# Weighted sum of expert rows moved to TensorE, bias and variance scaling moved from GpSimd to VectorE

## Chip, cores, metric

One core of one Trainium2 chip. The metric is the device time of one launch in microseconds; lower is better.

## The reference, cut to what matters

One layer of a streaming encoder for 1024 prompt frames and 64 sample frames (1088 rows of 1024 numbers, fp32). A mixer of retention and attention, then a hierarchical mixture of 16 experts in which every row goes to two experts, then a last layer norm:

```
combine[row, e] = weight of expert e for this row      # two of the 16 are not zero
ffn[row]  = sum over e of combine[row, e] * (silu(h @ w_gate[e]) * (h @ w_up[e])) @ w_down[e]
x[row]    = layer_norm(alpha * x1[row] + gate * ffn[row], ln_ffn_g, ln_ffn_b)
```

Here alpha is 2 ** 0.25, gate is a vector of 1024 (one for the prompt, one for the sample), and the layer norm subtracts the row's mean, multiplies by (variance + 1e-5) ** -0.5, then applies gain and bias.

## The kernel before

The program is written engine by engine, with explicit semaphores; each engine runs its own instructions in order. Earlier stages: modulation, projections, retention, attention, out projection, router. Then the experts work on blocks of 128 rows sorted by expert. ScalarE stores each block of expert results to DRAM (expert_rows, 512 KB a block, L1332).

The final stage is the one that is changed. It goes over nine tiles t of rows: eight of 128 and the last of 64. For tile t:

- GpSimd gathers, by two indirect DMAs (`gather`, L1854), the rows of the first and of the second chosen expert into ya[t] and yc[t]. Their landing counts on semaphore s_y0[t % 4].
- ScalarE multiplies ya[t] by the first weight w0 (L1345), and counts s_crs.
- VectorE adds w1 times yc[t] (L1758), multiplies by the gate row (L1759), adds alpha times x1 while it accumulates the row sum (L1760), and makes the negated mean (L1761), which counts s_cve.
- ScalarE squares the centred rows into yc and accumulates (L1350), s_csq.
- GpSimd scales that sum to variance plus epsilon (L1872), raises it to -0.5 (L1873), multiplies by the negated mean (L1874), s_cnm.
- ScalarE applies scale and shift (L1356), s_cxh; VectorE multiplies by the gain (L1766), s_cg; GpSimd adds the bias (L1879), s_cy; SyncE stores the tile (L749).

The order is fixed by three software pipelines, each a loop over t. VectorE, iteration t: the first part of tile t, then the gain of tile t-3. ScalarE: scaling of t, squares of t-1, application of t-3. GpSimd: gathers of tiles 0, 1, 2 ahead of the loop; in iteration t the gather of t+3 (from t = 1 on after the squares of t-1), the scalars of t-1, the bias of t-3.

TensorE has no work in this stage; its last instruction is L1113. `mm` (L762) is its matrix product helper, so products of all stages have the line L762. The wrapper `step` makes an engine wait for its own instruction; `done` does the same on a named semaphore.

Of the kernel before, what the change touches and what calls it, by code (L numbers as in the profile page):

```python
# [107 lines left out]
def rows_of(t):  # L108
    return P if t < LAST else DEC
# [18 lines left out]
def stream_step(nc, a):  # L128
# [5 lines left out]
    with ExitStack() as ctx:  # L134
# [75 lines left out]
        def tiny(*dims, dt=F32):  # L210
# [74 lines left out]
        gate_lin = view(r_tmp + 1024, 2, 512)  # L285


        s_rot, s_const, s_rows, s_router = sem("rotations_in"), sem("const_in"), sem("rows_in"), sem("router_in")
        s_xb = [sem(f"x_in{i}") for i in range(3)]
        s_adaB = [sem(f"ada_first_in{i}") for i in range(4)]  # L290
        s_adaM = [sem(f"ada_later_in{i}") for i in range(2)]
        s_win = [sem(f"win_in{i}") for i in range(2)]
        s_wout, s_state = sem("wout_in"), sem("state_in")
        s_dv, s_po = sem("dve_steps"), sem("pool_steps")
        s_pH, s_pL = sem("operand_high"), sem("operand_low")
        s_rowT, s_colv, s_csig, s_silu = [sem(n) for n in
# [39 lines left out]
        s_gu, s_sg, s_g1, s_a, s_at, s_aH, s_aL, s_yp, s_ye, s_ys = [sem(n) for n in  # L336
            ("gate_up_ready", "gate_sig", "gate_silu", "act_ready", "act_turned", "act_high", "act_low",
             "down_ready", "y_copied", "y_stored")]
        s_frow = sem("final_rows_in")
        s_y0 = [sem(f"y_gathered{i}") for i in range(4)]  # L340
        s_x1i = sem("x1_in")
        s_cve, s_crs, s_cnm, s_cxh, s_cg, s_cy = [sem(n) for n in
            ("fin_variance", "fin_first", "fin_shift", "fin_applied", "fin_gained", "fin_ready")]
        s_csq = sem("fin_squares")
        s_cacc, s_yo = sem("fin_sum"), sem("y_out")
        s_go = sem("queue_order")
        s_fill = sem("unused_rows_cleared")
# [156 lines left out]
        ya = [view(r_b + D * t, D) for t in range(TILES)]  # L504
        yc = [view(r_a + D * t, D) for t in range(TILES)]
        x1c = [view(r_m + D * t, D) for t in range(TILES)]


        rt = [r_tmp]
# [74 lines left out]
        def _(sp):  # L584
# [78 lines left out]
                                 ).then_inc(s_kc[1], 16)  # L663

            load_cache(0)
            sp.dma_start(wout, w_out[0].rearrange("(k p) n -> p k n", p=P)).then_inc(s_wout, 16)
            for pair in range(1, PAIRS):
                load_cache(pair)

# [51 lines left out]
            for slot, src in enumerate((mod_row(1, 0, 2), mod_row(1, 1, 2),  # L721
                                        ln_ffn_g[0].unsqueeze(0).to_broadcast([P, D]),
                                        ln_ffn_b[0].unsqueeze(0).to_broadcast([P, D]))):
                sp.dma_start(rows8[:, slot, :], src).then_inc(s_frow, 16)

            sp.wait_ge(s_route, 1)
            total = sp.value_load(table[0:1, 16:17], min_val=1, max_val=MAX_BLOCKS - 1)
# [30 lines left out]
        def _(pe):  # L758
# [245 lines left out]
            pe.wait_ge(s_ov, N_OUT + PAIRS)  # L1004
            pe.wait_ge(s_meA, 12)
            pe.wait_ge(s_meD, 12)
            pe.wait_ge(s_wout, 16)

            def h2_turned(t):
                r = rows_of(t)  # L1010
# [64 lines left out]
            with pe.Fori(0, EXPERTS // 2) as ee:  # L1075
                for k in range(2):
                    first = pe.value_load(table[0:1, bass.ds(2 * ee + k, 1)], min_val=0, max_val=MAX_BLOCKS - 1)
                    end = pe.value_load(table[0:1, bass.ds(2 * ee + k + 1, 1)], min_val=1, max_val=MAX_BLOCKS - 1)
                    with pe.Fori(first, end) as b:
                        pe.wait_ge(s_hL, b + 1)  # L1080
                        for half in range(2):
                            pe.wait_ge(s_wL, 12 * ee + 6 * k + 2 * half + 2)
                            for w in range(2):
                                cols = slice(half * 256, half * 256 + 256)
                                for c in range(KC):
                                    last = split_products(bank(half)[:, w * 256:w * 256 + 256], h_high[:, c, :],
                                                          h_low[:, c, :], high_w[w][:, c, cols], low_w[k][w][:, c, cols],
                                                          c == 0, c == KC - 1)
                            last.then_inc(s_gu, 1)
                        for half in range(2):  # L1090
                            pe.wait_ge(s_a, 2 * b + half + 1)
                            for f in range(2):
                                last = nc.tensor.transpose(bank(6 + half)[:, f * P:(f + 1) * P],  # L1093
                                                           an[:, half, f * P:(f + 1) * P], ident)
                            last.then_inc(s_at, 1)
                            if half == 0:
                                pe.wait_ge(s_hg, 16 * b + 32)
                                for c in range(KC):
                                    last = nc.tensor.transpose(psum[1][:, c // 4, (c % 4) * P:(c % 4 + 1) * P],
                                                               hg[:, c * P:(c + 1) * P], ident)  # L1100
                                last.then_inc(s_htr, 1)
                        pe.wait_ge(s_ye, b + 1)
                        pe.wait_ge(s_wL, 12 * ee + 6 * k + 6)
                        for f in range(FC):
                            if f % 2 == 0:
                                pe.wait_ge(s_aL, 2 * b + f // 2 + 1)
                            for hh in range(2):
                                cols = slice(hh * 512, hh * 512 + 512)
                                last = split_products(psum[2][:, hh, :], a_high[:, f, :], a_low[:, f, :],
                                                      high_w[2][:, f, cols], low_w[k][2][:, f, cols], f == 0, f == FC - 1)  # L1110
                        last.then_inc(s_yp, 1)

                    nc.tensor.transpose(bank(7)[0:64, 0:64], ident[0:64, 0:64], ident[0:64, 0:64]).then_inc(s_edone, 1)  # L1113


        @block.scalar
        def _(act):
# [222 lines left out]

            for t in range(TILES + 3):
                if t < TILES:
                    r = rows_of(t)
                    act.wait_ge(s_y0[t % 4], 32 * (t // 4 + 1))
                    A(ya[t][0:r], ya[t][0:r], ACT.Copy, scale=w0[0:r, t:t + 1]).then_inc(s_crs, 1)  # L1345
                v = t - 1
                if 0 <= v < TILES:
                    r = rows_of(v)
                    act.wait_ge(s_cve, v + 1)
                    A(yc[v][0:r], ya[v][0:r], ACT.Square, bias=fin_nm[0:r, v:v + 1],  # L1350
                      accum_out=fin_sq[0:r, v:v + 1]).then_inc(s_csq, 1)
                v = t - 3
                if v >= 0:
                    r = rows_of(v)
                    act.wait_ge(s_cnm, v + 1)
                    A(ya[v][0:r], ya[v][0:r], ACT.Identity, bias=ln_nmr[0:r, v:v + 1],  # L1356
                      scale=ln_rstd[0:r, v:v + 1]).then_inc(s_cxh, 1)
# [3 lines left out]
        def _(dve):  # L1361
# [386 lines left out]
            dve_pair(EXPERTS // 2 - 1, True)  # L1748


            dve.wait_ge(s_frow, 64)
            dve.wait_ge(s_x1i, 16 * TILES)
            for t in range(TILES + 3):
                if t < TILES:
                    r = rows_of(t)
                    x = ya[t][0:r]
                    dve.wait_ge(s_crs, t + 1)
                    step(STT(x, yc[t][0:r], w1[0:r, t:t + 1], x, ALU.mult, ALU.add))  # L1758
                    step(TT(x, x, rows8[0:r, int(t == LAST)], ALU.mult))  # L1759
                    done(STT(x, x1c[t][0:r], ALPHA, x, ALU.mult, ALU.add, accum_out=fin_nm[0:r, t:t + 1]), s_cacc, t + 1)  # L1760
                    done(TS(fin_nm[0:r, t:t + 1], fin_nm[0:r, t:t + 1], -1.0 / D, None, ALU.mult), s_cve, t + 1)  # L1761
                v = t - 3
                if v >= 0:
                    r = rows_of(v)
                    dve.wait_ge(s_cxh, v + 1)
                    TT(ya[v][0:r], ya[v][0:r], rows8[0:r, 2], ALU.mult).then_inc(s_cg, 1)  # L1766


        @block.gpsimd
        def _(pool):  # L1770
# [86 lines left out]
                    pool.indirect_dma_start(dst[0:r], None, y_dram,  # L1857
                                            bass.IndirectOffsetOnAxis(ap=slot_i[0:r, kk, t:t + 1], axis=0)).then_inc(s_y0[t % 4], 16)

            for t in range(3):  # L1860
                gather(t)
            pool.wait_ge(s_frow, 64)
            for t in range(TILES + 3):
                if t + 3 < TILES:
                    if t:
                        pool.wait_ge(s_csq, t)
                    gather(t + 3)
                v = t - 1
                if 0 <= v < TILES:
                    r, c = rows_of(v), slice(v, v + 1)  # L1870
                    pool.wait_ge(s_csq, v + 1)
                    step(G.tensor_scalar(fin_sq[0:r, c], fin_sq[0:r, c], 1.0 / D, EPS, ALU.mult, ALU.add))  # L1872
                    step(G.tensor_tensor(ln_rstd[0:r, c], fin_sq[0:r, c], mhalf[0:r, 0:1], ALU.pow))  # L1873
                    G.tensor_tensor(ln_nmr[0:r, c], fin_nm[0:r, c], ln_rstd[0:r, c], ALU.mult).then_inc(s_cnm, 1)  # L1874
                v = t - 3
                if v >= 0:
                    r = rows_of(v)
                    pool.wait_ge(s_cg, v + 1)
                    G.tensor_tensor(ya[v][0:r], ya[v][0:r], rows8[0:r, 3], ALU.add).then_inc(s_cy, 1)  # L1879


def launch_shapes():
# [31 lines left out]
```

## Time and profile before

| what | value |
|---|---|
| median of 3 runs | 1600.95 us (1599.82 to 1601.17) |
| profiled execution, span | 1600.7 us (its time as a whole isn't shown apart from the span) |
| TensorE busy | 1418.3 us, 89% |
| VectorE busy | 933.1 us, 58% |
| ScalarE busy | 612.9 us, 38% |
| GpSimd busy | 245.9 us, 15% |
| first gather of the final stage starts | 1520.66 us |

The engines are called PE (TensorE), PEld (its weight loads), DVE (VectorE), ACT (ScalarE), POOL (GpSimd) and SP (SyncE) in the rows. Busy shares are means over the whole span. The granted clock is the share of 2.4 GHz that TensorE was given; 0.50 is 1.2 GHz. A time in a row counts from the span's start unless it says otherwise.

### The profile page before, as it was taken

The page shows a single profiled execution, that of the slowest core. Times are in us where ns is not written, and L with a number is a line of the kernel's source. Part 1 is how long each engine was busy: PE and PEld are TensorE (multiplying, and loading weights), DVE is VectorE, ACT ScalarE, POOL GpSimd, SP SyncE. Part 2 cuts the span into 40 slices and gives each one's busy share as a digit, 9 for nine tenths or more (in the row PEclk, how much of TensorE's full clock was granted, in tenths as well). Part 3 has the DMA queues.
Part 4 walks back from the last instruction along what each step waited for, and adds up shares of the span by engine and source line. Part 5 has one row for each costly group of instructions (what it writes and reads, how often), then busy time and mean ns, then how long its engine had stood idle before and what let it go on. Part 6 is the DMA issues. An engine that isn't in the chain of part 4 may idle for free.

```text
span 1600.7 us, 20719 instructions
## 1 busy us (share of the span) xinstructions
PE 1418.3 (89%) x7419; PEld 1004.3 (63%) x7420; DVE 933.1 (58%) x1308; ACT 612.9 (38%) x1054; POOL 245.9 (15%) x239
## 2 busy tenths in 40 slices
PE   5989899998999999999999973799999999999800
PEld 1433333566777666666645543699888889998700
DVE  5486873134611288888745555455888451538676
ACT  0200000124222277777602223145777442437543
POOL 0123210001300000002014430100000000000078
PEclk9999999999999999999999995799999999999955
DMA  9614140101021441211263214555899551539663
GB/s 344 221 53 158 54 164 1 53 1 67 0 86 43 83 138 28 54 27 27 90 226 119 88 64 169 197 210 210 333 381 383 214 211 64 210 116 371 254 220 114
DMA packets 137844, 233.89 MB, mean 146 GB/s; under 512 B 56536, under 2 KB 58144, under 8 KB 137784
## 3 DMA queue, kind: packets, MB, share of 16 engines
q1 hardware_dynamic: 127656, 196.39, 35.2%
q0 software_dynamic: 6352, 23.07, 4.2%
q10 hardware_dynamic: 3776, 13.67, 2.1%
q8 instruction: 34, 0.56, 0.1%
q14 instruction: 26, 0.21, 0.0%
HBM read 197.42 MB, written 35.68 MB: 146 GB/s over the span
## 4 chain that ended last, share of the span: by engine, by line
PE 77%; DVE 12%; POOL 4%; DMA 2%; ACT 1%; issue 1%; SPq 1%; POOLq 0%; DVEq 0%; ACTq 0%
PE psum L762 72%; DVE arena L1512 4%; PE psum L949 3%; POOL arena L1879 1%; DMA arena<-in_w_ada_mix 1%; POOL arena L1857 1%; PE psum L1093 1%; DVE arena L1728 1%; DVE arena L1730 1%; ACT arena L1318 1%; POOL smalls L1873 1%; DVE arena L1513 1%; DVE smalls L1469 1%; DVE arena L1510 1%; PE psum L795 0%
## 5 line engine op out<-in xcount | busy, mean ns | idle before, releaser
L762 PE MATMUL psum<-arena 128*128 128x64 f32 (+10 forms) x1468 | 352.0, 386 | 10.4 <-DVE arena L1699 9.0
L762 PEld LDWEIGHTS psum<-arena 128*128 128x128 f32 (+3 forms) x1468 | 203.2, 189 | 98.5 <-issue 80.1
L762 PE MATMUL psum<-high,h_high 128*128 128x256 f32 x832 | 238.3, 286 | 2.5 <-DVE h_low L1715 2.5
L762 PE MATMUL psum<-high,h_low 128*128 128x256 f32 x832 | 236.6, 284 | 0.0
L762 PE MATMUL psum<-win,hT 128*128 128x512 f32 (+1 forms) x432 | 193.0, 601 | 0.5 <-ACT hT L1131 0.5
L762 PEld LDWEIGHTS psum<-high,h_high 128*128 128x128 f32 x832 | 160.8, 193 | 4.3 <-issue 2.9
L762 PEld LDWEIGHTS psum<-high,h_low 128*128 128x128 f32 x832 | 160.8, 193 | 0.0
L762 PEld LDWEIGHTS psum<-win,hT 128*128 128x128 f32 (+1 forms) x432 | 78.2, 185 | 110.8 <-issue 106.6
L1553 DVE TENSOR_TENSOR_SCAN arena<-arena 128x512 f32<-128x512 f32 (+4 forms) x116 | 115.3, 994 | 26.8 <-ACT arena L1241 24.9
L762 PE MATMUL psum<-low_even,h_high 128*128 128x256 f32 x416 | 118.9, 286 | 0.0
L762 PE MATMUL psum<-low_odd,h_high 128*128 128x256 f32 x416 | 117.7, 283 | 0.0
L1710 DVE TENSOR_TENSOR low_odd<-raw_odd,high 128x2048 fp32r<-128x2048 f32 x48 | 107.9, 2288 | 11.4 <-ACT high L1291 11.3
L1710 DVE TENSOR_TENSOR low_even<-raw_even,high 128x2048 fp32r<-128x2048 f32 x48 | 107.7, 2287 | 10.2 <-ACT high L1291 10.2
L1728 DVE TENSOR_TENSOR arena<-arena,psum 128x256 f32<-128x256 f32 x52 | 21.8, 419 | 145.7 <-ACT arena L1313 95.8
L762 PE MATMUL psum<-win_high,x_high 128*128 128x512 f32 (+1 forms) x216 | 86.8, 402 | 10.0 <-DVE win_low L1492 6.2
L1291 ACT ACTIVATE high<-raw_odd 128x2048 fp32r<-128x2048 f32 x48 | 89.2, 1911 | 6.1 <-ACT arena L1330 6.1
L1291 ACT ACTIVATE high<-raw_even 128x2048 fp32r<-128x2048 f32 x48 | 88.9, 1909 | 5.3 <-ACT arena L1330 5.3
L1512 DVE SCALAR_TENSOR_TENSOR arena<-arena,smalls 128x512 f32<-128x512 f32 x96 | 86.3, 899 | 3.4
L762 PE MATMUL psum<-win_low,x_high 128*128 128x512 f32 (+1 forms) x216 | 85.6, 396 | 0.0
L762 PE MATMUL psum<-win_high,x_low 128*128 128x512 f32 (+1 forms) x216 | 85.5, 396 | 0.0
L762 PE MATMUL psum<-high,a_high 128*128 128x512 f32 x208 | 83.2, 400 | 0.0
L762 PE MATMUL psum<-arena,smalls 128*2 128x512 f32 (+3 forms) x168 | 61.0, 474 | 25.0 <-DMA arena<-in_w_ada_mix 12.5
(227 smaller groups left out, 2301.2 us busy)
## 6 DMA issues: line engine op xcount, KB each, us to landing
raw_even<-in_w_e_gate SPq DMA_DIRECT2D x8, 2048.0 KB, 10.4
raw_even<-in_w_e_up SPq DMA_DIRECT2D x8, 2048.0 KB, 16.9
raw_even<-in_w_e_down SPq DMA_DIRECT2D x8, 2048.0 KB, 15.5
raw_odd<-in_w_e_gate SPq DMA_DIRECT2D x8, 2048.0 KB, 10.2
raw_odd<-in_w_e_up SPq DMA_DIRECT2D x8, 2048.0 KB, 16.3
raw_odd<-in_w_e_down SPq DMA_DIRECT2D x8, 2048.0 KB, 14.7
win<-in_w_in SPq DMA_DIRECT2D x7, 2048.0 KB, 9.2
expert_rows<-arena ACTq DMA_DIRECT2D x26, 512.0 KB, 6.7
```

The costliest lines, as they stand in the source:

```text
L762: pe_last[0] = nc.tensor.matmul(*x, **y)
L949: last = nc.tensor.transpose(bank(3 + u % 2)[0:r, j * P:(j + 1) * P], wgt[:, u % 3, j * P:j * P + r], ident)
L1093: last = nc.tensor.transpose(bank(6 + half)[:, f * P:(f + 1) * P], an[:, half, f * P:(f + 1) * P], ident)
L1291: A(chunk(high_w, c), chunk(raw_w[k], c), ACT.Copy).then_inc(s_wH, 1)
L1318: A(sg[:, 1], bank(1)[:, 0:256], ACT.Sigmoid).then_inc(s_sg, 1)
L1469: TT(rope_a[0:r].rearrange("p h (a d) -> p h a d", a=2), b4, cos, ALU.mult).then_inc(s_ra, 1)
L1510: step(TS(o, w[:, 0], silu_c[:, 0, st:st + 1], None, ALU.mult))
L1512: step(STT(o, w[:, k], silu_c[:, k, st:st + 1], o, ALU.mult, ALU.add))
L1513: done(STT(o, w[:, KC - 1], silu_c[:, KC - 1, st:st + 1], o, ALU.mult, ALU.add), s_acc, i + 1)
L1553: done(V.tensor_tensor_scan(pbr, om[:, u % 3, w - 1::-1], om[:, u % 3, w - 1::-1], init, ALU.mult, ALU.min), s_scan, u + 1)
L1710: TT(chunk(low_w[k], c), chunk(raw_w[k], c), chunk(high_w, c).bitcast(F32), ALU.subtract).then_inc(s_wL, 1)
L1728: TT(an[:, half], sg[:, half], bank(half)[:, 0:256], ALU.mult).then_inc(s_g1, 1)
```

## The change

TensorE makes the weighted sum: for each tile ScalarE writes two 128x128 matrices that hold w0 and w1 of the tile on their diagonal (the identity times a column), and TensorE multiplies them with the gathered rows, in fp32, into one of three PSUM buffers (psum 0, 2, 3, in turn). VectorE reads the sum from PSUM in its gate product. The variance scaling and the bias addition go from GpSimd to VectorE. The GpSimd loop is rewritten: gather t in iteration t, then the scalars of tile t-2. Two semaphores are merged with others: the final rows count on the router's, the output weights on the state's.

The core of the diff:

```
 TensorE, new, behind the experts:
+            for t in range(TILES):
+                r = rows_of(t)
+                pe.wait_ge(s_dg, 2 * t + 2)
+                pe.wait_ge(s_y0[t % 4], 32 * (t // 4 + 1))
+                if t >= 3:
+                    pe.wait_ge(s_cg, t - 2)
+                for hh in range(2):
+                    for kk, y in enumerate((ya[t], yc[t])):
+                        last = mm(fin_psum[t % 3][0:r, hh, :], row_weight[t % 2][0:r, kk, 0:r], y[0:r, hh * 512:hh * 512 + 512],
+                                  start=(kk == 0), stop=(kk == 1))
+                last.then_inc(s_crs, 1)
 ScalarE:
-                    act.wait_ge(s_y0[t % 4], 32 * (t // 4 + 1))
-                    A(ya[t][0:r], ya[t][0:r], ACT.Copy, scale=w0[0:r, t:t + 1]).then_inc(s_crs, 1)
+                    if t >= 2:
+                        act.wait_ge(s_crs, t - 1)
+                    for kk, w in enumerate((w0, w1)):
+                        A(row_weight[t % 2][:, kk], ident, ACT.Copy, scale=w[:, t:t + 1]).then_inc(s_dg, 1)
 VectorE:
                     dve.wait_ge(s_crs, t + 1)
-                    step(STT(x, yc[t][0:r], w1[0:r, t:t + 1], x, ALU.mult, ALU.add))
-                    step(TT(x, x, rows8[0:r, int(t == LAST)], ALU.mult))
+                    done(TT(x, fin_psum[t % 3][0:r].rearrange("p a b -> p (a b)"), rows8[0:r, int(t == LAST)], ALU.mult),
+                         s_cg, t + 1)
                     done(STT(x, x1c[t][0:r], ALPHA, x, ALU.mult, ALU.add, accum_out=fin_nm[0:r, t:t + 1]), s_cacc, t + 1)
                     done(TS(fin_nm[0:r, t:t + 1], fin_nm[0:r, t:t + 1], -1.0 / D, None, ALU.mult), s_cve, t + 1)
+                v = t - 1
+                if 0 <= v < TILES:
+                    r, c = rows_of(v), slice(v, v + 1)
+                    dve.wait_ge(s_csq, v + 1)
+                    TS(fin_sq[0:r, c], fin_sq[0:r, c], 1.0 / D, EPS, ALU.mult, ALU.add).then_inc(s_cvar, 1)
                 v = t - 3
                 if v >= 0:
                     dve.wait_ge(s_cxh, v + 1)
-                    TT(ya[v][0:r], ya[v][0:r], rows8[0:r, 2], ALU.mult).then_inc(s_cg, 1)
+                    step(TT(ya[v][0:r], ya[v][0:r], rows8[0:r, 2], ALU.mult))
+                    TT(ya[v][0:r], ya[v][0:r], rows8[0:r, 3], ALU.add).then_inc(s_cy, 1)
 GpSimd:
-            for t in range(3):
-                gather(t)
-            pool.wait_ge(s_frow, 64)
-            for t in range(TILES + 3):
-                if t + 3 < TILES:
-                    if t:
-                        pool.wait_ge(s_csq, t)
-                    gather(t + 3)
-                v = t - 1
-                if 0 <= v < TILES:
+            for t in range(TILES + 2):
+                if t < TILES:
+                    if t >= 4:
+                        pool.wait_ge(s_crs, t - 3)
+                    gather(t)
+                v = t - 2
+                if v >= 0:
                     r, c = rows_of(v), slice(v, v + 1)
-                    pool.wait_ge(s_csq, v + 1)
-                    step(G.tensor_scalar(fin_sq[0:r, c], fin_sq[0:r, c], 1.0 / D, EPS, ALU.mult, ALU.add))
+                    pool.wait_ge(s_cvar, v + 1)
                     step(G.tensor_tensor(ln_rstd[0:r, c], fin_sq[0:r, c], mhalf[0:r, 0:1], ALU.pow))
                     G.tensor_tensor(ln_nmr[0:r, c], fin_nm[0:r, c], ln_rstd[0:r, c], ALU.mult).then_inc(s_cnm, 1)
-                v = t - 3
-                if v >= 0:
-                    r = rows_of(v)
-                    pool.wait_ge(s_cg, v + 1)
-                    G.tensor_tensor(ya[v][0:r], ya[v][0:r], rows8[0:r, 3], ALU.add).then_inc(s_cy, 1)
```

## Rows read from the trace of the kernel before

**Rows 1.** Head of the page: span, then busy us by engine.

```profile
span 1600.7 us, 20719 instructions
PE 1418.3 (89%) x7419; PEld 1004.3 (63%) x7420; DVE 933.1 (58%) x1308; ACT 612.9 (38%) x1054; POOL 245.9 (15%) x239
```

**Rows 2.** Chain of waits, 1480 to 1601: start us, us, what.

```profile
1520.66 0.94 POOL arena L1857
...
1521.90 5.30 DMA arena<-expert_rows,smalls
...
1594.39 2.29 POOLq L134
```

**Rows 3.** Busy time by stretch: PE, PEld, DVE, ACT, POOL, clock, DMA share, GB/s.

```profile
1540.00:1550.00 10.00, 0.00 (x0) 0.00 (x0) 9.65 (x15) 7.17 (x9) 8.68 (x10) 0.50 0.46 138
```

**Rows 4.** Groups, shapes apart, 1516 to 1601: busy us, mean ns, idle before.

```profile
L1857 POOL DMA_INDIRECT arena<-expert_rows,smalls x18 | 21.0, 1168 | 36.2 <-DMA expert_rows<-arena 28.5 <-issue 4.2 <-ACT arena L1350 3.6
L1879 POOL TENSOR_TENSOR arena<-arena 128x1024 f32<-128x1024 f32 x8 | 20.7, 2596 | 0.0
```

**Rows 5.** Timeline, 1515 to 1601: start us, us, engine, line, operation.

```profile
1529.83 1.23 DVE L1759 TENSOR_TENSOR arena<-arena 128x1024 f32<-128x1024 f32 x1
...
1532.36 0.15 DVE L1761 TENSOR_SCALAR smalls<-smalls 128x1 f32<-128x1 f32 x1
...
1539.64 0.79 POOL L1874 TENSOR_TENSOR smalls<-smalls 128x1 f32<-128x1 f32 x1
...
1541.95 0.94 POOL L1857 DMA_INDIRECT arena<-expert_rows,smalls  x1 [0.30 <-issue]
...
1543.34 1.57 POOL L1873 TENSOR_TENSOR smalls<-smalls 128x1 f32<-128x1 f32 x1
...
1546.01 1.24 ACT L1356 ACTIVATE arena<-arena,smalls 128x1024 f32<-128x1024 f32 x1
...
1546.13 1.90 POOL L1857 DMA_INDIRECT arena<-expert_rows,smalls  x1 [0.16 <-ACT arena L1350]
...
1549.77 0.57 POOL L1873 TENSOR_TENSOR smalls<-smalls 128x1 f32<-128x1 f32 x1
...
1575.27 3.41 DVE L1760 SCALAR_TENSOR_TENSOR arena<-arena 64x1024 f32<-64x1024 f32 x1
...
1584.32 0.19 POOL L1874 TENSOR_TENSOR smalls<-smalls 128x1 f32<-128x1 f32 x1
...
1588.78 7.91 POOL L1879 TENSOR_TENSOR arena<-arena 128x1024 f32<-128x1024 f32 x3
```

**Rows 6.** Line 1857, the two gathers issued at 1546.13 and 1548.34.

```profile
DMA to landing us min/median/max: 5.2/5.3/5.4
```

**Rows 7.** Timeline of weight loads in the out projection, 806 to 811.

```profile
809.47 0.33 PEld L762 LDWEIGHTS psum<-arena 128*128 128x128 f32 x1 [0.52 <-issue]
810.32 0.19 PEld L762 LDWEIGHTS psum<-arena 128*128 128x128 f32 x1 [0.51 <-issue]
810.75 0.19 PEld L762 LDWEIGHTS psum<-arena 128*128 128x128 f32 x1 [0.24 <-issue]
```

**Rows 8.** Busy time by short stretch; the third number from the end is the clock.

```profile
386.00:387.00 1.00, 0.78 (x2) 0.72 (x3) 1.00 (x3) 1.00 (x3) 0.00 (x0) 0.50 1.05 387
...
390.00:391.00 1.00, 1.00 (x4) 0.80 (x4) 1.00 (x2) 0.00 (x0) 0.00 (x0) 0.77 0.45 172
...
1012.00:1014.00 2.00, 1.49 (x7) 1.50 (x8) 2.00 (x2) 1.27 (x1) 0.29 (x1) 0.50 1.06 238
...
1018.00:1019.00 1.00, 1.00 (x8) 1.00 (x8) 0.97 (x1) 0.00 (x0) 0.00 (x0) 0.74 1.04 418
...
1520.00:1521.00 1.00, 0.00 (x0) 0.00 (x0) 0.00 (x0) 0.00 (x0) 0.34 (x1) 0.64 0.00 0
```

**Rows 9.** Line 1739 (ns min/median/max), and a group of ScalarE (us, ns).

```profile
L1739 DVE TENSOR_TENSOR h_low<-psum,h_high x26: 1224/1225/1227, 1030.1 to 1511.4; 128x1024 fp32r<-128x1024 f32 x26
...
L1212 ACT ACTIVATE arena<-psum 128x128 f32<-128x128 f32 x32 | 8.9, 277 | 4.9 <-PE psum L762 4.9
```

More of the change, by code:

```diff
@@ L285, in stream_step @@
         gate_lin = view(r_tmp + 1024, 2, 512)
-        s_rot, s_const, s_rows, s_router = sem("rotations_in"), sem("const_in"), sem("rows_in"), sem("router_in")
+        s_rot, s_const, s_rows, s_router = sem("rotations_in"), sem("const_in"), sem("rows_in"), sem("router_then_final_rows_in")
         s_xb = [sem(f"x_in{i}") for i in range(3)]
@@ L292, in stream_step @@
         s_win = [sem(f"win_in{i}") for i in range(2)]
-        s_wout, s_state = sem("wout_in"), sem("state_in")
+        s_state = sem("state_then_wout_in")
         s_dv, s_po = sem("dve_steps"), sem("pool_steps")
@@ L338, in stream_step @@
              "down_ready", "y_copied", "y_stored")]
-        s_frow = sem("final_rows_in")
         s_y0 = [sem(f"y_gathered{i}") for i in range(4)]
@@ L344, in stream_step @@
         s_csq = sem("fin_squares")
+        s_cvar, s_dg = sem("fin_variance_scaled"), sem("row_weights_ready")
         s_cacc, s_yo = sem("fin_sum"), sem("y_out")
@@ L506, in stream_step @@
         x1c = [view(r_m + D * t, D) for t in range(TILES)]
+        fin_psum = [psum[0], psum[2], psum[3]]
+        row_weight = [view(r_b + D * TILES + 256 * i, 2, P) for i in range(2)]
         rt = [r_tmp]
@@ L665, in _ @@
             load_cache(0)
-            sp.dma_start(wout, w_out[0].rearrange("(k p) n -> p k n", p=P)).then_inc(s_wout, 16)
+            sp.dma_start(wout, w_out[0].rearrange("(k p) n -> p k n", p=P)).then_inc(s_state, 16)
             for pair in range(1, PAIRS):
@@ L723, in _ @@
                                         ln_ffn_b[0].unsqueeze(0).to_broadcast([P, D]))):
-                sp.dma_start(rows8[:, slot, :], src).then_inc(s_frow, 16)
+                sp.dma_start(rows8[:, slot, :], src).then_inc(s_router, 16)
             sp.wait_ge(s_route, 1)
@@ L1006, in _ @@
             pe.wait_ge(s_meD, 12)
-            pe.wait_ge(s_wout, 16)
+            pe.wait_ge(s_state, 32)
             def h2_turned(t):
@@ L1342, in _ @@
                 if t < TILES:
-                    r = rows_of(t)
-                    act.wait_ge(s_y0[t % 4], 32 * (t // 4 + 1))
-                    A(ya[t][0:r], ya[t][0:r], ACT.Copy, scale=w0[0:r, t:t + 1]).then_inc(s_crs, 1)
+                    if t >= 2:
+                        act.wait_ge(s_crs, t - 1)
+                    for kk, w in enumerate((w0, w1)):
+                        A(row_weight[t % 2][:, kk], ident, ACT.Copy, scale=w[:, t:t + 1]).then_inc(s_dg, 1)
                 v = t - 1
@@ L1748, in _ @@
             dve_pair(EXPERTS // 2 - 1, True)
-            dve.wait_ge(s_frow, 64)
+            dve.wait_ge(s_router, 128)
             dve.wait_ge(s_x1i, 16 * TILES)
```

## The prediction, made before the changed kernel was run

> **What bounds the kernel now.** Read the head of the page first [rows 1]: TensorE is busy 89% of the span, GpSimd 15%. That average says nothing of the stage that is changed, because TensorE has finished when it begins. So read next the chain of waits from 1517 us to the end [rows 2]: after the gather of tile 0 (landing at 1527.2) it goes from one GpSimd line to the next, the last one a closing wait at 1594.39. The stage is 80.0 us long, from the first gather's start at 1520.66 to 1600.7. The stretch 1540 to 1550 [rows 3] shows VectorE 9.65 and GpSimd 8.68 of 10 us busy, ScalarE 7.17, TensorE nothing and a granted clock of 0.50. The groups of the stage [rows 4] say what fills GpSimd: 18 gathers (21.0 us) and the bias additions of L1879 (20.7 us in 8, the ninth 2.3). The timeline [rows 5] shows VectorE and GpSimd holding each other up: the 128x1 power L1873 takes 1.57 us beside VectorE work and 0.57 alone, a gather 1.90 or 0.94. So the stage is bound by GpSimd, with VectorE close behind.
>
> **Outside the stage** only semaphores are shared differently (output weights with the state, final rows with the router). Each old wait keeps its position and its transfer, so I take 0. The later count cannot be passed early, since its transfers are issued behind the earlier ones; cover would be missing only if they landed out of order.
>
> **Costs inside the stage, by engine.**
> GpSimd loses 9 bias additions (2.3 to 3.4 us each) and 9 one-column scalings. Per tile it keeps two gathers and two one-column operations: 0.57+0.07+0.19 = 0.85 us with VectorE idle, 1.57+0.07+0.79 = 2.4 us beside it [rows 5].
> VectorE loses the weighted sum L1758 and gets the bias addition (1.23 as L1759) and the scaling (0.15 as L1761). Its gate product now reads PSUM; the nearest row, 128x1024 from PSUM, has 1.225 us [rows 9]. Up to the negated mean an iteration takes 1.25+1.25+0.2 = 2.7 us (1529.83 to 1532.52); with the variance scaling 2.9; gain and bias of the tile three back 2.5. That is 5.4 us per tile.
> ScalarE's 1.15 us scaling becomes two of 128x128. The nearest row, 128x128 from PSUM without a scale column, has 0.277 us [rows 9]; bounds are that and 1.15, the operation replaced; I take 0.3. They are written an iteration ahead, during the gather's flight; uncovered, 0.3 to 2.3 us a tile.
> TensorE gets, per tile, four products 128x128 by 128x512 in fp32. The weight loads of the out projection (16 such products a tile, two records each) show the pace [rows 7]: 0.85 us per record at 1.2 GHz (809.47, 810.32), 0.43 at 2.4 (810.32, 810.75). Eight records are 3.4 us fast or 6.8 slow, plus some 0.2 to the last result. Which clock applies: from 1520.3 it is at half, some 4 us after the last product, with TensorE idle all that time [rows 8]. After restarts at half it came back 4.2 us later (from 386.2, busy 0.78 of that slice, to about 390.5) and 6.0 us later (1012.5 to 1018.5). I take the first, as its products are as wide as the new ones. In 4.2 us slow 4.9 records pass, the other 3.1 take 1.3: 5.5, with the last result 5.7 us for a tile after a long gap; bounds 3.6 and 7.0.
>
> **The new wait.** This decides the forecast. In the new GpSimd program gather t stands behind the scalars of tile t-3, and these wait for the scaled variance of t-3. VectorE issues that scaling inside iteration t-2, behind its own wait for TensorE's tile t-2. In the old program gather t was held only by the squares of t-4, and the first four pairs went out at once; now three do. A new round therefore holds two tiles: from VectorE's start on tile t-2 through scaling, scalars, gather t, landing and products to its start on tile t. Landing is 5.3 us from the second gather's start [rows 6] (5.2 to 5.4). Tile t+1 follows inside the same round, its gather issued behind the next scalars.
> With VectorE busy on an older tile's gain and bias, a round is
> 2.9 (to the scaled variance) + 0.05 + 2.4 (scalars) + 0.15 + 2.1 (first gather 1.8, gap 0.3) + 5.3 + 5.7 = 18.6 us.
> VectorE's own work for these two tiles is only 10.8. Even from lowest values, 2.9+0.05+0.85+0.15+1.25+5.2+3.6 = 14.0, the round is longer than that: the wait binds whichever bound is right. TensorE idles 9 us in each round, so it starts slow again. The highest is 2.9+0.05+2.4+0.15+2.2+5.4+7.0 = 20.1.
>
> The Trainium skill, "SBUF — State Buffer", section Who interferes with whom, infers that a two-input VectorE operation does not hold up the writing of gather descriptors. Here the gather beside VectorE took 1.90 us against 0.94 [rows 5], so the trace disagrees. By the page the first gather would take 0.95 in each of the two busy rounds, and the sum would be 1.7 us less, 1610.7; the measurement decides.
>
> **The sum**, in us from the span's start:
> - Tile 0 lands at 1527.2 as before; products slow at first, +5.7, 1532.9; tile 1 at +3.4, 1536.3, and tile 2 at 1539.7. VectorE has finished tile 0's first part (1535.5) and starts tile 1 there.
> - First round, to tile 3: no older tile's gain and bias in the way, so scalars 0.85 and first gather with gap 1.25: 2.9+0.05+0.85+0.15+1.25+5.3+5.7 = 16.2, 1552.5. Tile 2 fits inside.
> - Two full rounds, to tiles 5 and 7: 37.2, 1589.7.
> - From VectorE's start on tile 7: 2.9+2.5 for it with tile 4's gain and bias, 2.9+2.5 for tile 8 with tile 5's, 0.2 for the last scaling, 7.5 for gain and bias of 6, 7 and 8: 18.5, 1608.2. ScalarE's application for 8 is over before VectorE gets there (scaling 1600.7, scalars 2.4, application 1.24: 1604.4, gain at 1605.7).
> - From the last row operation to the end as now: 1588.78+7.91 = 1596.7 to 1600.7, 4.0. Span 1612.2.
> The profiled execution's span is 0.25 us below the median of the runs; no separate total of it is shown, so I add the difference: 1612.4, said as 1612.
>
> **Rivals.**
> B. Same round, but cheaper: the clock does not fall in the gaps (three rounds by 2.1 us, 1606), or GpSimd's small operations are unobstructed (scalars 1.55 and gather 0.85 shorter in each of two rounds, 4.8 together, 1607.6), or both, 1601. For: VectorE idles much of a round, so there is less to collide with. Against: the fall in [rows 8] after a shorter idle than 9 us, and the 1.57 and 1.90 us of [rows 5].
> C. The other side: gathers arrive in time and the relieved GpSimd pays off. Then VectorE starts tile 3 at 1542.6 (2.9 after tile 2) and every tile costs 5.4 us, or GpSimd's 3.1+2.4+0.2 = 5.7; start on tile 8 at 1542.6+5x5.7 = 1571.1, then 2.9+2.5+0.2+7.5 and 4.0: 1588, 13 us faster. For: the stage's bound engine loses over 30 us of work, and VectorE no longer meets L1879 (3.41 us instead of 1.22 in the worst). Against: landing and products would have to fit into the 10.8 us that VectorE is busy per two tiles; from that point on C holds, and the lowest round is 14.0. C needs a misreading of the order of waits.
> D. The products stay at 1.2 GHz through each whole first tile: 1.3 us more at the start and in each of three rounds, 5.2: 1617.6. For: the 6.0 us restart. Against: the 4.2 us one. With the first round obstructed like the others too (2.4 more), 1620.
>
> **Numbers.** Forecast A (1607 to 1617) 0.60; B (1601 to 1607) 0.16, its 1607.6 corner counted with A; C 0.12; D 0.12. The three old runs lie between 1599.8 and 1601.2, so about 0.2%, 3.2 us, can be told from no change. C is faster, 0.12. Half of B lies within 3.2 us, 0.08. The rest is slower, 0.80. The range 1603 to 1619 leaves out C, the bottom quarter of B and the top third of D, 0.20 in all. Forecast: slower by 0.7%, 1612.
>
> **What would show it.** Right: four pairs of gathers no longer start together, the fourth begins after the first scaled variance, near 1541; VectorE waits for TensorE before tiles 3, 5 and 7, 5 to 8 us each, and hardly before 4, 6 and 8; the starts of tiles 3, 5 and 7 lie 18 us apart; granted clock half at each such start; no VectorE operation of the stage above 1.3 us; last row operation on VectorE near 1608. Wrong: VectorE over 90% busy through the stage (C); a granted clock of 1.0 at the start of tile 5 (B); spacing above 20 us (D); any shift of the first gather by over 1 us, which would mean that the shared semaphores cost something outside the stage.

## The result, and the profile after

The changed kernel takes 1612.6 us (median of 4 runs), the one before 1601.1. The ratio is 1.0074 with a 95% interval of 1.0059 to 1.0090: slower by 0.7%, 11.5 us. The medians, here and in the table of the experiments, count every execution, while the ratios leave out the slow ones (here 1644.9 us after and 1632.1 before, one of four each).

The profiled execution has a span of 1610.1 us, some 2.1 below its own time; its final stage begins 1.6 us earlier than in the trace of before. So the stages are compared from the first gather to the end of the span: 91.1 us after (1519.03 to 1610.1), 80.0 before. That difference is 11.1 us. The spans differ by 9.4, because of the earlier beginning; such a shift comes without the change too (see Signs in the section on the prediction).

Head of the page of the changed kernel, span and busy us by engine (compare [rows 1]):

```profile
span 1610.1 us, 20872 instructions
PE 1456.4 (90%) x7491; PEld 1019.5 (63%) x7492; DVE 923.2 (57%) x1317; ACT 607.9 (38%) x1063; POOL 215.3 (13%) x221
```

TensorE got 38 us more, the other three have less to do. GpSimd lost 31 us of work, VectorE 10, ScalarE 5, and the kernel is slower. Busy time went down and waiting went up, as the waits of the changed kernel's stage show (who waited for whom: us in total, times, the longest):

```profile
ACT arena L1365 <- DVE smalls L1776: 58.9, 9, 16.7
...
DVE arena L1773 <- PE psum L764: 48.8, 6, 20.2
POOL smalls L1890 <- DVE smalls L1781: 42.3, 6, 11.5
```

The waits form a ring: VectorE waits for TensorE, TensorE for GpSimd's gathers, GpSimd for VectorE's scaled variance (L1781). ScalarE waits beside it, for VectorE. The longest wait of each is the one for the first tile (8.0 us of VectorE's and 1.8 of ScalarE's lie ahead of the stage); the rest recurs. Where three engines of a stage of 91 us wait 41 to 57 us of it each, the time lies in the latency of the ring and in no engine's work.

One round in the timeline, from VectorE's start on tile 3 to its start on tile 5 (start us, us, engine, line, operation, idle before):

```profile
1551.23 1.23 DVE L1773 TENSOR_TENSOR arena<-psum,arena 128x1024 f32<-128x1024 f32 x1 [8.75 <-PE psum L764]
...
1553.95 0.15 DVE L1781 TENSOR_SCALAR smalls<-smalls 128x1 f32<-128x1 f32 x1
...
1554.19 1.48 POOL L1890 TENSOR_TENSOR smalls<-smalls 128x1 f32<-128x1 f32 x1 [8.36 <-DVE smalls L1781]
...
1555.75 0.79 POOL L1891 TENSOR_TENSOR smalls<-smalls 128x1 f32<-128x1 f32 x1
...
1556.71 1.02 POOL L1878 DMA_INDIRECT arena<-expert_rows,smalls  x1 [0.16 <-issue]
...
1558.03 1.67 POOL L1878 DMA_INDIRECT arena<-expert_rows,smalls  x1 [0.31 <-issue]
...
1564.08 10.12 PE L764 MATMUL psum<-arena 128*128 128x512 f32 x16 [9.45 <-issue]
...
1570.81 1.23 DVE L1773 TENSOR_TENSOR arena<-psum,arena 128x1024 f32<-128x1024 f32 x1 [9.14 <-PE psum L764]
```

Follow the releases: VectorE scales the variance of tile 2 (1553.95) only once tile 3's first part is done; GpSimd makes the scalars of tile 2, then issues tile 5's gathers (1556.71, 1558.03); TensorE gets them at 1564.08, and VectorE, idle for 9.14 us, starts tile 5 at 1570.81. In [rows 3] VectorE was busy 9.65 of 10 us; there the gathers ran ahead. The gap before the products is put down to "issue", since the landing is not named; it is the flight of the second gather, from its start at 1558.03 to its landing 6.0 us later.

Ahead of tile 3 (products from 1545.40) the profile names another releaser, ScalarE's matrices (L1360). Those are the matrices of tile 4: tile 3's had been written by 1539.23. Tile 3's second gather began at 1539.98 and landed 5.3 us later, at 1545.3, so there too the gather is what TensorE waited for.

Busy time by short stretch (as in [rows 8]; the third number from the end is the granted clock) around the products of tile 5:

```profile
1562.00:1564.00 2.00, 0.00 (x0) 0.00 (x0) 0.00 (x0) 0.08 (x1) 1.70 (x2) 0.50 0.96 367
1564.00:1570.00 6.00, 5.92 (x7) 2.52 (x8) 0.00 (x0) 0.00 (x0) 0.13 (x1) 0.50 0.58 193
1570.00:1572.00 2.00, 2.00 (x6) 0.86 (x5) 1.19 (x1) 0.00 (x0) 0.00 (x0) 0.96 0.00 0
```

Behind 9.45 us of idle TensorE starts at 1.2 GHz and is still there six us later, when the tile is nearly done.

### The profile page after: what moved, and what is told of

It is laid out like the page before. It is cut to its first block, busy times and chain, and to the rows that moved or that the text cites. A ratio compares the mean times of both kernels' runs of the same rounds, so it can differ in the third digit from the quotient of the medians.

```text
span 1610.1 us, 20872 instructions
## 1 busy us (share of the span) xinstructions
PE 1456.4 (90%) x7491; PEld 1019.5 (63%) x7492; DVE 923.2 (57%) x1317; ACT 607.9 (38%) x1063; POOL 215.3 (13%) x221
## 4 chain that ended last, share of the span: by engine, by line
PE 78%; DVE 14%; DMA 2%; ACT 2%; issue 1%; SPq 1%; POOL 1%; DVEq 0%; POOLq 0%; ACTq 0%
PE psum L764 73%; DVE arena L1527 4%; PE psum L951 3%; DMA arena<-in_w_ada_mix 1%; PE psum L1095 1%; DVE arena L1743 1%; DVE arena L1745 1%; ACT arena L1332 1%; DVE arena L1775 1%; DVE arena L1773 1%; DVE arena L1528 1%; DVE arena L1787 1%; DVE smalls L1484 1%; DVE arena L1525 1%; DVE arena L1786 0%
## 5 line engine op out<-in xcount | busy, mean ns | idle before, releaser
L764 PE MATMUL psum<-arena 128*128 128x64 f32 (+6 forms) x1540 | 392.9, 403 | 47.8 <-issue 18.8
L764 PEld LDWEIGHTS psum<-arena 128*128 128x128 f32 (+3 forms) x1540 | 219.2, 191 | 160.1 <-issue 133.0
L1725 DVE TENSOR_TENSOR low_odd<-raw_odd,high 128x2048 fp32r<-128x2048 f32 x48 | 107.9, 2288 | 11.5 <-ACT high L1305 11.4
```

The lines of the kernel that those rows point to most:

```text
L764: pe_last[0] = nc.tensor.matmul(*x, **y)
L1725: TT(chunk(low_w[k], c), chunk(raw_w[k], c), chunk(high_w, c).bitcast(F32), ALU.subtract).then_inc(s_wL, 1)
```

## The experiments

The theory, called O in the expectations: GpSimd's order puts each gather behind scalars that wait, through VectorE's scaled variance, for a tile that itself waits for an earlier gather. Rivals: P, the fp32 products on TensorE with their slow clock; V, the work that VectorE took over. Times are medians; ratios are to the kernel before, run beside them on the same chip, with 95% intervals.

| kernel | us | ratio |
|---|---|---|
| changed kernel | 1612.6 | 1.0074 (1.0059 to 1.0090) |
| e1, gathers ahead | 1588.2 | 0.9919 (0.9900 to 0.9939) |
| e2, old sum, late gathers | 1648.1 | 1.0304 (1.0284 to 1.0324) |
| e3, scaling ahead of the wait | 1597.8 | 0.9990 (0.9977 to 1.0003) |
| e4, scaling on GpSimd | 1595.9 | 0.9973 (0.9962 to 0.9984) |
| e5, products at full clock | 1604.4 | 1.0023 (1.0013 to 1.0033) |
| e6, e1 with bias on GpSimd | 1596.7 | 0.9979 (0.9950 to 1.0007) |
| e7, e1 with the old sum | 1590.5 | 0.9935 (0.9916 to 0.9955) |
| e10, e2 with bias later | 1612.3 | 1.0064 (1.0040 to 1.0088) |
| e8, e1 with weights ahead | 1585.2 | 0.9904 (0.9884 to 0.9923) |
| e9, e8 with filler | 1583.0 | 0.9886 (0.9869 to 0.9904) |

### e1: the gathers ahead

```
-            for t in range(TILES + 2):
-                if t < TILES:
-                    if t >= 4:
-                        pool.wait_ge(s_crs, t - 3)
-                    gather(t)
-                v = t - 2
-                if v >= 0:
+            for t in range(4):
+                gather(t)
+            for v in range(TILES):
+                if v + 4 < TILES:
+                    pool.wait_ge(s_crs, v + 1)
+                    gather(v + 4)
+                if True:
 ...
```

> The changed kernel, but GpSimd issues the gathers of tiles 0 to 3 at once and the gather of tile v+4 ahead of the scalars of tile v (it waits for the products of tile v, as the semaphore demands). All arithmetic and all other engines are those of the changed kernel. Theory O (the order on GpSimd makes a round of two tiles that lasts 18 to 19 us): the round is gone, VectorE starts tiles 3 to 8 some 5.2 to 5.7 us apart without waits, the stage shrinks from 91 to 67 to 71 us, time 1588 (1586 to 1594). Theory P (the fp32 products on TensorE, slow after each gap, are what costs): the products remain, gain under 9 us, time 1603 or more. Theory V (VectorE has too much work since it took bias and scaling): no change, 1612.

Measured 1588.2 us. Not an operation was added or taken away, and 24 us are gone: 11.5 that the change cost and 13 more. Theory O holds. P and V fall as main causes: all products and all of VectorE's new work are still there. So is the slow clock, in part: in e1's chain the products of tiles 4 and 6 take 5.4 us each, with a granted clock of 0.68 from 1544 to 1548 and 0.58 from 1555 to 1559. Two of VectorE's starts in e1's timeline, tiles 4 and 5:

```profile
1549.84 1.23 DVE L1773 TENSOR_TENSOR arena<-psum,arena 128x1024 f32<-128x1024 f32 x1 [2.47 <-PE psum L764]
...
1555.02 1.22 DVE L1773 TENSOR_TENSOR arena<-psum,arena 128x1024 f32<-128x1024 f32 x1
```

They lie 5.2 us apart, without a wait ahead of tile 5. The expectation that no waits stay was too good: 2.47 us do ahead of tile 4, and 6.5 in all behind tile 0. e8 takes them up.

### e3 and e4: cutting the tie, not the order

e3 moves one VectorE operation within its iteration:

```
             for t in range(TILES + 3):
+                v = t - 1
+                if 0 <= v < TILES:
+                    r, c = rows_of(v), slice(v, v + 1)
+                    dve.wait_ge(s_csq, v + 1)
+                    TS(fin_sq[0:r, c], fin_sq[0:r, c], 1.0 / D, EPS, ALU.mult, ALU.add).then_inc(s_cvar, 1)
                 if t < TILES:
...
-                v = t - 1
-                if 0 <= v < TILES:
-                    r, c = rows_of(v), slice(v, v + 1)
-                    dve.wait_ge(s_csq, v + 1)
-                    TS(fin_sq[0:r, c], fin_sq[0:r, c], 1.0 / D, EPS, ALU.mult, ALU.add).then_inc(s_cvar, 1)
```

> The changed kernel, with one operation moved: in VectorE's iteration t the scaling of the variance of t-1 stands ahead of the wait for TensorE's tile t, not behind the first part of tile t. GpSimd's order is left as it is. Theory O with the tie that the prediction named (the scaled variance of t-3 waits for VectorE's start on t-2): a round now holds three tiles and lasts 18 to 20 us, 6.1 to 6.7 us a tile instead of 9.3; starts on tiles 3 and 6 some 20 us apart; time 1598 (1595 to 1603). If the lateness of the gathers alone counts and not this tie: under 3 us gained. Theories P and V: 1612.

e4 gives the scaling back to GpSimd, which waits for ScalarE's squares instead:

```
 VectorE:
-                    dve.wait_ge(s_csq, v + 1)
-                    TS(fin_sq[0:r, c], fin_sq[0:r, c], 1.0 / D, EPS, ALU.mult, ALU.add).then_inc(s_cvar, 1)
 GpSimd:
-                    pool.wait_ge(s_cvar, v + 1)
+                    pool.wait_ge(s_csq, v + 1)
+                    step(G.tensor_scalar(fin_sq[0:r, c], fin_sq[0:r, c], 1.0 / D, EPS, ALU.mult, ALU.add))
```

> The changed kernel with one part undone: the variance scaling is on GpSimd again, behind the squares, not on VectorE. Bias on VectorE, sum on TensorE and the order of the gathers as in the change. Theory O: the tie to VectorE's iteration is gone, a round holds three tiles, and GpSimd pays 0.4 to 1.1 us more per tile; time 1598 (1594 to 1604), so that giving GpSimd work back makes the kernel faster. Theory V: VectorE saves 0.15 us a tile, 1611. Theory P: 1612 to 1615.

Measured 1597.8 and 1595.9 us, as theory O has it and neither rival: the gathers stand where the change put them, and 15 and 17 us come back. VectorE's starts on tiles 3, 5 and 6 in e3:

```profile
1549.70 1.23 DVE L1778 TENSOR_TENSOR arena<-psum,arena 128x1024 f32<-128x1024 f32 x1 [4.70 <-PE psum L764]
...
1560.04 1.21 DVE L1778 TENSOR_TENSOR arena<-psum,arena 128x1024 f32<-128x1024 f32 x1
1566.20 1.22 DVE L1778 TENSOR_TENSOR arena<-psum,arena 128x1024 f32<-128x1024 f32 x1 [0.91 <-PE psum L764]
```

Three tiles now pass in 16.5 us, where the changed kernel needs 19.6 for two. I had expected 18 to 20. VectorE's own work for three tiles is 15.5 us, so the ring hardly binds any more. One more thing than the tie changed in e3: the scalars now stand beside the gate product, which reads PSUM, and the power takes 0.57 us and the product 0.18 (from 1555.05), not 1.48 and 0.79. e4 is the cleaner test of the tie, since its scalars with the scaling still take 2.1 us (1553.12 to 1555.24). In e4, giving the engine that bound the stage before 9 operations more makes the kernel 17 us faster than the changed one: a small operation costs by what it waits for, not by its 0.15 us.

### e2 and e10: the order without the rest of the change

e2 is the kernel before with the late gathers alone:

```
-            for t in range(3):
-                gather(t)
             pool.wait_ge(s_frow, 64)
             for t in range(TILES + 3):
-                if t + 3 < TILES:
-                    if t:
-                        pool.wait_ge(s_csq, t)
-                    gather(t + 3)
-                v = t - 1
+                if t < TILES:
+                    if t >= 4:
+                        pool.wait_ge(s_crs, t - 3)
+                    gather(t)
+                v = t - 2
                 if 0 <= v < TILES:
...
                 v = t - 3
                 if v >= 0:
...
```

> The kernel before, with nothing of the change but the place of the gathers: gather t in iteration t of the GpSimd loop, behind the scalars of tile t-3, and the scalars one iteration later. Weighted sum on ScalarE and VectorE, bias and scaling on GpSimd, as before. Theory O: a round of two tiles is 1.15 + 1.35 (scaling of the rows, squares) + 3.2 (scalars) + 2.3 (a bias) + 2.1 + 5.3 = 15.4 us, against some 10.5 of work; slower than before, 1606 (1602 to 1612). Here no scaled variance on VectorE is in the round, so it costs less than in the changed kernel. Theories P and V: no TensorE in the stage and VectorE as before, so 1601.

Measured 1648.1 us, 48 slower than before (1600.4 beside it) where I expected 5. The direction is that of theory O, the size refutes my reckoning of the round. Its chain of waits says why (start us, us, what):

```profile
1563.51 1.24 DVE arena L1766
...
1564.81 2.34 POOL arena L1877
...
1567.32 1.06 POOL arena L1857
...
1568.68 5.29 DMA arena<-expert_rows,smalls
...
1573.99 1.16 ACT arena L1345
...
1575.18 1.30 DVE arena L1758
```

I had only counted the scalars' wait. The bias (L1877) of tile t-3 also stands ahead of gather t+1, and it waits for the gain of t-3 (L1766), which VectorE makes behind the first part of tile t. So gather t+1 waits for tile t to be there: a round of one tile, and ScalarE's starts on new tiles are 15.7 us apart (1558.29 and 1573.99 in this trace). e10 tests this by moving the bias one iteration:

```
-            for t in range(TILES + 3):
+            for t in range(TILES + 4):
...
-                v = t - 3
+                v = t - 4
                 if v >= 0:
                     r = rows_of(v)
                     pool.wait_ge(s_cg, v + 1)
```

> e2 with one thing different: GpSimd's bias addition one iteration later (tile t-4 in iteration t). In e2 the gather of tile t+1 stands behind the bias of t-3, which waits for the gain of t-3, and that comes on VectorE behind the first part of tile t: a round of one tile, 15.8 us. Here the bias does not wait for the newest tile any more, only the scalars tie gather t to tile t-2: a round of two tiles, about 15.4 us, 7.7 a tile. Time 1608 (1602 to 1616), 40 us under e2. If something else made e2 slow: over 1640.

Measured 1612.3 us, 36 back from one index. It has rounds of two tiles, 17.4 us from tile 3 to tile 5 and 16.3 from there to tile 7. VectorE's starts on tiles 3, 4 and 5:

```profile
1546.76 1.28 DVE L1758 SCALAR_TENSOR_TENSOR arena<-arena,smalls 128x1024 f32<-128x1024 f32 x1 [6.33 <-ACT arena L1345]
1551.93 1.28 DVE L1758 SCALAR_TENSOR_TENSOR arena<-arena,smalls 128x1024 f32<-128x1024 f32 x1
1564.12 1.28 DVE L1758 SCALAR_TENSOR_TENSOR arena<-arena,smalls 128x1024 f32<-128x1024 f32 x1 [4.92 <-ACT arena L1345]
```

Late gathers cost the old arithmetic 11 us without any TensorE in the stage, about what the change cost. With the bias where it stood, this order costs 48 us. So the change needed the bias either off GpSimd, as it has it, or one iteration later, as e10 has it, for its order to cost no more than 11.

### e5: the clock

```
 TensorE, ahead of the waits of tile t:
+                if t >= 3:
+                    pe.wait_ge(s_cg, t - 2)
+                for _ in range({0: 12, 3: 6, 5: 10, 7: 10}.get(t, 0)):
+                    mm(fin_psum[t % 3][:, 0, :], ident, cst[:, 0:512], start=True, stop=True)
```

> The changed kernel, with filler products on TensorE (fp32 128x512, results overwritten) in its idle stretches: 12 ahead of tile 0, 6 ahead of tile 3, 10 ahead of tiles 5 and 7, so that the granted clock is at its upper level when the gathered rows land. Order on GpSimd unchanged. Theory O: only the slow parts of tiles 0, 3, 5 and 7 go (5.4, 5.8, 6.7 and 5.5 us in the changed kernel's trace, 3.6 each at the upper level): 9 us less, 1603.5 (1601 to 1607), still slower than before, with rounds of 16.5 us. Theory P (the clock is the cause): time at or under 1597.

Measured 1604.4 us: 8 of the expected 9 us, and still slower than before (interval 1.0013 to 1.0033). The chain around tile 7 has the products at the upper level, 3.69 us, behind a flight of 6.58 us:

```profile
1568.77 6.58 DMA arena<-expert_rows,smalls
...
1575.48 3.69 PE psum L764 x8
...
1579.19 1.24 DVE arena L1775
```

The rounds to tiles 5 and 7 are 17.0 and 17.2 us, not 16.5; the one to tile 7 lost 0.6 in the longer flight (6.0 in the changed kernel). The clock thus holds 8 us of the stage, but as a consequence: TensorE is slow where the round has left it idle.

### e6 and e7: the two moves, with the order out of the way

e6 is e1 with GpSimd adding the bias (two tiles behind, with a wait for the final rows ahead of its loop):

```
 VectorE:
-                    step(TT(ya[v][0:r], ya[v][0:r], rows8[0:r, 2], ALU.mult))
-                    TT(ya[v][0:r], ya[v][0:r], rows8[0:r, 3], ALU.add).then_inc(s_cy, 1)
+                    TT(ya[v][0:r], ya[v][0:r], rows8[0:r, 2], ALU.mult).then_inc(s_gained, 1)
 GpSimd, behind the scalars of v:
+                u = v - 2
+                if u >= 0:
+                    r = rows_of(u)
+                    pool.wait_ge(s_gained, u + 1)
+                    G.tensor_tensor(ya[u][0:r], ya[u][0:r], rows8[0:r, 3], ALU.add).then_inc(s_cy, 1)
```

> The kernel of e1 (gathers ahead) with the bias addition undone: GpSimd adds the bias again, two tiles behind. VectorE falls to 4.0 us a tile, GpSimd rises to 3.1 + 2.4 + 2.3 = 7.8 us a tile while it gathers. If the move of the bias to VectorE is a gain by itself: slower than e1 by 8 to 15 us, 1600 (1595 to 1606). If VectorE's load is what counts: equal to e1 or faster, 1588 or less.

e7 is e1 with the old sum (TensorE's new loop is taken out as well):

```
 ScalarE:
-                    for kk, w in enumerate((w0, w1)):
-                        A(row_weight[t % 2][:, kk], ident, ACT.Copy, scale=w[:, t:t + 1]).then_inc(s_dg, 1)
+                    act.wait_ge(s_y0[t % 4], 32 * (t // 4 + 1))
+                    A(ya[t][0:r], ya[t][0:r], ACT.Copy, scale=w0[0:r, t:t + 1]).then_inc(s_crs, 1)
 VectorE:
-                    done(TT(x, fin_psum[t % 3][0:r].rearrange("p a b -> p (a b)"), rows8[0:r, int(t == LAST)], ALU.mult), s_cg, t + 1)
+                    step(STT(x, yc[t][0:r], w1[0:r, t:t + 1], x, ALU.mult, ALU.add))
+                    step(TT(x, x, rows8[0:r, int(t == LAST)], ALU.mult))
```

> The kernel of e1 with the weighted sum undone: ScalarE scales the first rows, VectorE adds the second, no TensorE in the stage; bias and variance scaling stay on VectorE. VectorE rises from 5.2 to 6.5 us a tile, but its start on tile 0 comes 1.3 us after the landing, not 5.6, and the waits for TensorE (6.5 us in e1 behind tile 0) go: start on tile 8 at the same time as in e1. If the products buy nothing net: 1589 (1585 to 1594). If taking the sum from VectorE is worth its 1.3 us in all nine tiles: 1598 or more.

Measured 1596.7 and 1590.5 us. Having the bias on VectorE is worth some 8 us (e1 against e6, intervals apart). The products are not worth anything that these runs tell: 1588.2 against 1590.5, with overlapping intervals. TensorE takes 1.3 us a tile from VectorE, 11.9 in all (6.49 us a tile in e7, 5.17 in e1 where nothing is waited for), and gives nearly all of it back. VectorE starts tile 0 12.2 us after the first gather's start in e1 and 7.7 in e7, and e1 has 6.5 us of waits behind it.

### e8 and e9: a faster version

e8 writes the matrices of tile t+1 in ScalarE's iteration t (`row_weights` is the loop over the two matrices that is taken out below):

```
+            row_weights(0)
             for t in range(TILES + 3):
-                if t < TILES:
-                    if t >= 2:
-                        act.wait_ge(s_crs, t - 1)
-                    for kk, w in enumerate((w0, w1)):
-                        A(row_weight[t % 2][:, kk], ident, ACT.Copy, scale=w[:, t:t + 1]).then_inc(s_dg, 1)
+                if t + 1 < TILES:
+                    if t >= 1:
+                        act.wait_ge(s_crs, t)
+                    row_weights(t + 1)
```

> The kernel of e1, and ScalarE writes the weight matrices of tile t+1 in its iteration t, ahead of the squares and the application of older tiles (it waits for the products of tile t-1, whose buffer it takes). In e1 TensorE waited for ScalarE's matrices ahead of four tiles (8.2 us) and VectorE for TensorE 6.5 us behind tile 0. Most of that goes: 4 us less than e1, 1584 (1582 to 1587).

e9 is e8 with e5's filler ahead of tile 0 alone.

> The kernel before this one in the list, with the 12 filler products ahead of tile 0 alone, so that the first tile is multiplied at the upper clock: 3.6 us instead of 5.4. 2 us less again, 1582 (1580 to 1585). If the clock matters not at all here: equal.

Measured 1585.2 and 1583.0 us, 3 and then 2 less, about as expected. The intervals of e1 and e8 overlap, and so do those of e8 and e9, so each step by itself rests on the medians and on the traces: the stage lasts 68.9 us in e1, 63.9 in e8 and 62.4 in e9, and VectorE starts tile 0 12.0 us after the first gather's start in e8, 10.5 in e9. e9 beats both kernels, by 18 us (before) and 30 us (changed). VectorE's starts on tiles 4 to 6 in e9:

```profile
1544.99 1.22 DVE L1779 TENSOR_TENSOR arena<-psum,arena 128x1024 f32<-128x1024 f32 x1
1550.16 1.22 DVE L1779 TENSOR_TENSOR arena<-psum,arena 128x1024 f32<-128x1024 f32 x1
1555.34 1.22 DVE L1779 TENSOR_TENSOR arena<-psum,arena 128x1024 f32<-128x1024 f32 x1
```

5.17 us apart, no wait: the stage is bound by VectorE's work from tile 4 on. Against e7 with its 1590.5 the sum on TensorE is now worth 7.5 us, the filler's 2 among them (ratios 0.9886 and 0.9935, intervals apart).

## Why the prediction was right

The sum, term by term, from the first gather's start; the last column is read from the changed kernel's timeline:

| term | forecast us | measured us |
|---|---|---|
| to VectorE's start on tile 1 | 15.6 | 15.65 |
| round to tile 3 | 16.2 | 16.55 |
| round to tile 5 | 18.6 | 19.6 |
| round to tile 7 | 18.6 | 18.3 |
| from there to the last row operation's end | 18.5 | 17.6 |
| to the end of the span | 4.0 | 3.4 |
| stage | 91.5 | 91.1 |

The ends of these terms, where they are not among the rows above (the round to tile 3 begins at 1534.68; 1605.51 is the last row operation):

```profile
1519.03 0.94 POOL L1878 DMA_INDIRECT arena<-expert_rows,smalls  x1 [28.41 <-DMA expert_rows<-arena]
...
1534.68 1.23 DVE L1773 TENSOR_TENSOR arena<-psum,arena 128x1024 f32<-128x1024 f32 x1 [0.72 <-PE psum L764]
...
1589.11 1.22 DVE L1773 TENSOR_TENSOR arena<-psum,arena 128x1024 f32<-128x1024 f32 x1 [7.87 <-PE psum L764]
...
1605.51 1.22 DVE L1787 TENSOR_TENSOR arena<-arena 64x1024 f32<-64x1024 f32 x1
```

- **The new wait** was the right step, and e1, e3 and e4 show it as the cause: without the order or without the tie the loss becomes a gain or nothing.
- **The total is closer than it deserves.** Forecast 1612.4, measured 1612.6. The stage was forecast within 0.4 us, but two further errors cancel. The forecast takes the stage's start from the trace of before, and in the changed kernel's it lies 1.6 us earlier. And it adds 0.25 us from the span to the time, where the execution with the span 1610.1 took 1612.22. That part of the agreement is luck.
- **Terms of the busy rounds.** Scalars 2.4 (measured 2.44 in the round to tile 5, from 1554.10), scaled variance 2.9 (2.87): right. The two gathers were taken wrongly, with errors that cancel. I put the delay on the first one, 2.1 us to the second's start; it was 1.32. The second was held up instead, 1.67 us for 0.94, and its rows came that much later, 6.05 us after its start and not 5.3. Together 7.4 forecast, 7.37 measured. The round to tile 5 is 1.0 us longer than forecast by its products alone (6.7 for 5.7). The end was taken too long by 0.9: a tile takes VectorE 5.17 us and not 5.4, gain and bias 2.4 and not 2.5.
- **Who holds the gather up.** The Trainium skill, "SBUF — State Buffer", section Who interferes with whom, says that a VectorE operation with at most one SBUF input, outside its two-port modes, leaves GpSimd alone. The trace agrees: the gather at 1576.28 took 1.02 us beside the gate product, which reads PSUM and one row table. I had carried over 1.90 us from a time when both inputs were in SBUF [rows 5]. The second gather of that tile began inside L1775, two SBUF inputs, and took 1.67 us; that contradicts again the inference in that section of the Trainium skill that such operations don't delay gathers.

```profile
1575.99 1.22 DVE L1773 TENSOR_TENSOR arena<-psum,arena 128x1024 f32<-128x1024 f32 x1
...
1576.28 1.02 POOL L1878 DMA_INDIRECT arena<-expert_rows,smalls  x1 [0.16 <-issue]
...
1577.24 1.23 DVE L1775 SCALAR_TENSOR_TENSOR arena<-arena 128x1024 f32<-128x1024 f32 x1
...
1577.60 1.67 POOL L1878 DMA_INDIRECT arena<-expert_rows,smalls  x1 [0.30 <-issue]
```

- **The products** after a gap: 5.7 forecast, 5.4, 5.8, 6.7 and 5.5 measured for tiles 0, 3, 5 and 7. Rival D's long restart came once in four, ahead of tile 5, and even there the clock rose before the tile's end.
- **What lay hidden** stayed so but once: ScalarE's matrices, 0.34 us each against my 0.3, made TensorE wait 1.3 us ahead of tile 2. That fell inside the first round and cost nothing.
- **Rivals.** B's clock is worth 8 us with the start included (e5); its price of 2.1 us for each of the four slow tiles makes 8.4. C, 1588, described a kernel with the gathers in time, and e1 is that kernel, with 1588.2. So close a match is partly luck: C's stage would last 67.5 us and e1's lasts 68.9, with 5.2 us a tile instead of C's 5.7 and 6.5 us of waits that C did not have. C failed for the reason given, the order of waits. V had not been among the rivals and is refuted by e1.
- **Signs.** Two of them came out otherwise. VectorE's waits before tiles 3, 5 and 7 were 8.8, 9.1 and 7.9 us, not 5 to 8; the forecast's own round of 18.6 us less 10.8 of work makes 7.8 already. And the first gather began 1.6 us earlier, where a shift of over 1 us was to mean that the shared semaphores cost something. That sign was too fine. With the program ahead of the stage unchanged, the first gather starts at 1520.66 in the kernel before, 1520.52 in e10 and 1517.19 in e2; with the changed program it starts at 1519.03, in e1 at 1518.20 and in e3 at 1520.32. A shift of 1.6 us tells nothing within that scatter.
- **Outside the stage** no trace shows a cost: the last wait before the stage, for the stored expert rows, is 28.4 us, against 28.5 in [rows 4].

Left open: how the 11.5 us divide between the order and the products. e10 loses 11 us by late gathers with no product in the stage, and e5 gives 8 back with the order left in place, but their rounds hold different operations and do not add up.

## What to carry to other kernels

Before counting what an engine saves, write down for each prefetch which instruction stands ahead of it on its queue and what that one waits for, through every engine, until you come back to a prefetch. The tiles between the two are the depth of the pipeline; the latency of the ring divided by the depth is the time of a tile. If that is above the busiest engine's work, moving work off that engine buys only what it takes out of the ring. Issue transfers ahead of dependent small operations, and look at a tiny operation's place before its size: one operation of 0.15 us a tile held 15 us here, one index of the bias 36.

## What the runs showed that was not expected

- A change of order alone can outweigh all arithmetic of a stage: with the same instructions, 1612.6 and 1588.2 us; with the old arithmetic, 1601, 1612.3 and 1648.1 us for three places of gathers and bias.
- TensorE's restart at the lower level lasted through nearly a whole tile once: at 1.2 GHz from 1564.08 to about 1570.1, six us, with products back to back, where the same products were at the upper level 3.4 us after 1525.77. No run shows why.
- The filler products do what they are for: in e5 the rows of tile 7 were multiplied in 3.69 us. Whether they are free is not shown. The rows of tile 7 landed 6.58 us after the second gather's start, and 6.0 us after it in the changed kernel.
- What holds a gather up is the two-input VectorE operation under way when it begins. In the trace of before, the gather at 1546.13 began inside the operation below, which ends at 1547.12, and was done 0.91 us after that end, although the next such operation had begun; alone it takes 0.94. The one at 1541.95 began 0.02 us after L1759 (1541.93 to 1543.20) and took 0.94 beside it. In the changed kernel the gathers at 1558.03 and 1577.60 were done 0.8 us after the end of the operation that they began in, and so was the one at 1543.96 in e1. This is read from a few rows; no run tests it.

```profile
1545.84 1.28 DVE L1758 SCALAR_TENSOR_TENSOR arena<-arena,smalls 128x1024 f32<-128x1024 f32 x1
```
